# Latent attention in paired turns, weight splits and pool copies at other places, transposes for the modulation rows, and a negated maximum

## The reference, cut to what matters

```python
def mla_pool_mixer(hc, hl, ...):
    al = attention(ql, concat([kc, kl]), concat([vc, vl]))         # x: 256 queries, 512 keys
    ol = concat([al, multiscale_pool(pl[..., i_p:], w_pool, s_pool)]) @ w_out
    ac = attention(qc, kc, vc)                                     # context: 256 queries, 256 keys
    oc = concat([ac, multiscale_pool(pc[..., i_p:], w_pool, s_pool)]) @ w_out
def attention(q, k, v):
    s = einsum('bqhgd,bkhd->bhgqk', q, k) * scale
    return einsum('bhgqk,bkhd->bqhgd', softmax(s), v)
def first_block(...):
    h = h + rms_norm(y, g_mix_post[i]); u = rms_norm(h, g_ffn_pre[i])       # a "join"
    ml = (silu(c) @ w_mod[i] + b_mod[i]).reshape(B, N_MOD, 1, D)            # modulation
```

## Time and profile before

| what | value |
|---|---|
| median of three executions | 1772.74 us |
| the profiled execution, its own time | 1771.68 us |
| its span, first to last instruction | 1769.9 us |
| TensorE busy | 1672.9 us, 95% |
| VectorE busy | 1215.4 us, 69% |
| ScalarE busy | 918.9 us, 52% |
| mean granted TensorE clock | 0.989 |
| latent attention, first scores to first product behind it | 924.0 to 993.4 us |

### The profile page before, as it was taken

The page is one execution under the profiler, slowest core; times in us unless marked ns, Lnnn a source line. Parts: engine busy times, 40 slices in busy tenths (PEclk is TensorE's granted clock), DMA queues, the critical chain, the costliest instruction groups (busy, mean ns, idle before and its releaser), DMA issues.

```text
span 1769.9 us, 25025 instructions
## 1 busy us (share of the span) xinstructions
PE 1672.9 (95%) x9848; PEld 1414.4 (80%) x9848; DVE 1215.4 (69%) x1462; ACT 918.9 (52%) x1192; POOL 0.2 (0%) x4
## 2 busy tenths in 40 slices
PE   7978999999998899999988999999999988999998
PEld 6867888988876788898864668888888867789997
DVE  6956778777875777756567459777666656677754
ACT  6476664474437665467466453331234264665543
POOL 0000000000000000000000000000000000000000
PEclk9999999999999999999998999999999999999999
DMA  7812558745651466633140126446544522045551
GB/s 251 297 56 96 172 184 259 236 153 194 202 167 49 127 190 227 212 120 111 51 123 21 49 72 202 155 130 227 205 147 158 171 86 96 29 139 191 188 176 66
DMA packets 240471, 264.75 MB, mean 150 GB/s; under 512 B 7007, under 2 KB 218978, under 8 KB 240354
## 3 DMA queue, kind: packets, MB, share of 16 engines
q1 hardware_dynamic: 238428, 258.84, 44.9%
q10 hardware_dynamic: 1926, 4.32, 0.7%
HBM read 262.08 MB, written 1.05 MB: 149 GB/s over the span
## 4 chain that ended last, share of the span: by engine, by line
PE 75%; ACT 12%; DVE 10%; issue 2%; DMA 0%; ACTq 0%; DVEq 0%
PE ps L728 74%; DVE wlo L1822 2%; ACT whi L1203 2%; ACT y L1608 1%; DVE pr L2374 1%; ACT u L1611 1%; DVE small L2363 1%; DVE y L2125 1%; ACT pr L1753 1%; PE ps L1134 1%; ACT u L1399 0%; ACT y L1339 0%; ACT sbl L1714 0%; ACT sbe L1710 0%; ACT sbt L1708 0%
## 5 line engine op out<-in xcount | busy, mean ns | idle before, releaser
L728 PE MATMUL ps<-u,whi 128*128 128x512 f32 (+1 forms) x3472 | 895.1, 341 | 25.8 <-DVE wlo L1822 7.4
L728 PEld LDWEIGHTS ps<-u,whi 128*128 128x128 f32 x3472 | 596.5, 190 | 123.1 <-issue 23.5
L728 PE MATMUL ps<-u,wlo 128*128 128x256 f32 (+1 forms) x2116 | 648.9, 307 | 0.0
L1822 DVE TENSOR_TENSOR wlo<-raw,whi 128x2048 fp32r<-128x2048 f32 (+6 forms) x212 | 454.0, 2142 | 213.5 <-ACT whi L1203 206.0
L1203 ACT ACTIVATE whi<-raw 128x2048 fp32r<-128x2048 f32 (+6 forms) x212 | 380.7, 1796 | 221.3 <-PE ps L728 203.0
L728 PEld LDWEIGHTS ps<-u,wlo 128*128 128x128 f32 x2116 | 402.3, 190 | 19.7
L728 PE MATMUL ps<-hid,whi 128*128 128x512 f32 (+1 forms) x1212 | 353.6, 364 | 0.0
L728 PE MATMUL ps<-hid,wlo 128*128 128x256 f32 (+1 forms) x864 | 261.6, 303 | 0.0
L728 PEld LDWEIGHTS ps<-hid,whi 128*128 128x128 f32 x1212 | 216.3, 189 | 40.3 <-issue 3.4
L728 PEld LDWEIGHTS ps<-hid,wlo 128*128 128x128 f32 x864 | 163.4, 189 | 7.1
L2125 DVE SCALAR_TENSOR_TENSOR y<-idle_half,cc,y 128x1024 f32<-128x1024 f32 x70 | 90.0, 1285 | 5.3 <-DVE wlo L1822 0.5
(11 more groups left out here) (269 smaller groups left out, 1619.3 us busy)
## 6 DMA issues: line engine op xcount, KB each, us to landing
raw<-in_ffn_w_up SPq DMA_DIRECT2D x44, 1024.0 KB, 5.1
raw<-in_w_ff_in SPq DMA_DIRECT2D x32, 1024.0 KB, 5.3
raw<-in_w_ff_out SPq DMA_DIRECT2D x32, 1024.0 KB, 5.3
modw<-in_w_mod SPq DMA_DIRECT2D x112, 256.0 KB, 3.9
idle_half<-in_w_mod SPq DMA_DIRECT2D x80, 256.0 KB, 3.5
raw<-in_w_in_dil SPq DMA_DIRECT2D x18, 1024.0 KB, 5.1
raw<-in_w_in_sb SPq DMA_DIRECT2D x12, 1024.0 KB, 7.3
raw<-in_w_ple_gate SPq DMA_DIRECT2D x8, 1024.0 KB, 5.0
```

The source lines that it names most:

```text
L728: return pe.matmul(out_, lhsT, rhs, start=start, stop=stop, skip_group_check=True)
L1822: nc.vector.tensor_tensor(wlo[:, s % SPLIT, 0:n], raw[:, c["r"] % RAW, 0:n], whi[:, s % SPLIT, 0:n].bitcast(F32), ALU.subtract).then_inc(* ...
```

## The change

1. The matrix `select` goes; `mod_turn` makes four 128x128 transposes with the identity into the whole bank, and VectorE reads every 32nd column of it. The constants' DMA is a ninth smaller.
2. `late_splits`: the split three ahead of `uv`'s last chunk is left until behind the latent attention; so two splits wait there in place of one.
3. In a join whose waiting splits hold the second chunk of the next product (`second_chunk`), ScalarE makes that chunk's `whi` before the join's first step. This holds at three joins: behind `ff_out0`, `dil_out` and `ff_out1`. VectorE's order stays.
4. The pool's four banks are copied inside the latent attention, two behind the first round's exponentials and maxima, one in each of the next two rounds.
5. The latent attention's rounds alternate: context, x, context, x.
6. The score's scale is put into q (in the copy of `uq`, and in the gain of `gqa`'s q), so the exponential has none, and the maximum is written negated: L2365 goes, 48 times.

```diff
-    squares = np.concatenate([ident, ones, negtri, -ones, perm1, perm_m, perm_g, past, select], axis=1)
+    squares = np.concatenate([ident, ones, negtri, -ones, perm1, perm_m, perm_g, past], axis=1)
...
+            if p["kind"] == "linear" and p["name"] == "uv":
+                return [], [p["groups"][-1][-1]["s"] + SPLIT]
...
-            return [], [s + 2, s + SPLIT] if p["name"] == "dil_out" else [s + SPLIT]
+            return [], [s + 2, s + SPLIT] if p["name"] in ("dil_out", "pool_w") else [s + SPLIT]
...
+        def second_chunk(i):
+
+            if phases[i]["kind"] != "join":
+                return None
+            q = phases[i + 1] if phases[i + 1]["evac"] != "ple" else phases[i + 2]
+            return q["groups"][1][0]["s"]
...
-                n = 0
-                for seg in (1, 0):
-                    for pair in range(4):
-                        for q in range(2):
+                for pair in range(4):
+                    for q in range(2):
+                        for seg in (1, 0):
+                            n = 2 * pair + 1 - seg
...
-                    last = mm(ps[:, 6, 4 * j:4 * j + 4], modrow[:, j * P:(j + 1) * P], select, True, True)
+                    last = pe.transpose(ps[:, 6, j * P:(j + 1) * P], modrow[:, j * P:(j + 1) * P], ident)
...
-                    nc.scalar.activation(qm[0:96, 2 * g:2 * g + 2, :], A_[0:96], ACT.Copy).then_inc(*up("group_read_s", key))
+                    nc.scalar.activation(qm[0:96, 2 * g:2 * g + 2, :], A_[0:96], ACT.Copy, scale=MLA_HD ** -0.5).then_inc(*up("group_read_s", key))
...
+                    if second_chunk(i) in waiting_splits(i):
+                        split_high(second_chunk(i))
                     for g in range(4):
                         act.wait_ge(*at("tiles_ready", (i, g)))
...
                     for u in units[0:step]:
                         exp_(u)
+                    if p["what"] == "mla":
+                        pool_high(i, 0)
+                        pool_high(i, 1)
                     for n in range(0, N, step):
                         for u in units[n + step:n + 2 * step]:
                             exp_(u)
+                        if p["what"] == "mla" and n < 4:
+                            pool_high(i, 2 + n // 2)
...
+                gain_q = vec[:, ROW["gqa_g_q"]:ROW["gqa_g_q"] + 1]
+                dve.wait_ge(*own())
+                nc.vector.tensor_scalar(gain_q, gain_q, P ** -0.5, None, ALU.mult).then_inc(*up("vector_step"))
...
-                            nc.vector.tensor_reduce(small[:, 8 + b:9 + b], ps[:, n % 4, 0:W], AX.X, ALU.max).then_inc(*up("vector_step"))
-                            dve.wait_ge(*own())
-                            nc.vector.tensor_scalar(small[:, b:b + 1], small[:, 8 + b:9 + b], -u["scale"], None, ALU.mult).then_inc(
-                                *up("max_ready", (i, n)))
+                            nc.vector.tensor_reduce(small[:, b:b + 1], ps[:, n % 4, 0:W], AX.X, ALU.max, negate=True).then_inc(*up("max_ready", (i, n)))
...
+                    if p["what"] == "mla":
+                        pool_low(0)
+                        pool_low(1)
```

More of the change, by code:

```diff
@@ L73, in constants @@
     past = (i[:, None] < i[None, :]).astype(float)
-    select = np.zeros((P, P))
-    for q in range(4):
-        select[32 * q, q] = 1.0
-    squares = np.concatenate([ident, ones, negtri, -ones, perm1, perm_m, perm_g, past, select], axis=1)
+    squares = np.concatenate([ident, ones, negtri, -ones, perm1, perm_m, perm_g, past], axis=1)
     freq = np.zeros((P, 1))
@@ L183, in build @@
         small = sb("small", [P, 64])
-        ident, ones, negtri, negones, perm1, perm_m, perm_g, past, select = (squares[:, j, :] for j in range(9))
-        select = select[:, 0:4]
+        ident, ones, negtri, negones, perm1, perm_m, perm_g, past = (squares[:, j, :] for j in range(8))
         ps = ctx.enter_context(nc.psum_tensor("ps", [P, 8, 512], F32))
@@ L532, in build @@
         latent_i = next((p["i"] for p in phases if p["kind"] == "cnorm"), None)
+        pool_group = next((p["groups"][0][0]["gi"] for p in phases if p.get("evac") == "poolw"), None)
         entry_i = next((p["i"] for p in phases if p["kind"] == "entry"), None)
@@ L630, in softmax_units @@
                 u["n"] = n
-                u["ends"] = n + 1 == len(units) or units[n + 1]["pair"] != u["pair"]
+                u["ends"] = all(v["pair"] != u["pair"] for v in units[n + 1:])
             return units
@@ L1501, in evac @@
                 elif kind == "poolw":
-                    for t in range(4):
-                        act.wait_ge(*own())
-                        nc.scalar.activation(uh[:, 4 + t, :], ps[:, 4 + t, :], ACT.Copy, scale=vec[:, ROW["pool_scale_2"] + t:ROW["pool_scale_2"] + t + 1]).then_inc(
-                            *up("operand_high", (i, t)))
+                    pass
                 elif kind == "conv" and g % 2 == 0:
@@ L1524, in evac, with pool_high @@
                         hidden_high_conv(p, g)
+            def pool_high(i, t):
+                act.wait_ge(*own())
+                nc.scalar.activation(uh[:, 4 + t, :], ps[:, 4 + t, :], ACT.Copy, scale=vec[:, ROW["pool_scale_2"] + t:ROW["pool_scale_2"] + t + 1]).then_inc(
+                    *up("operand_high", ("pool", t)))
             def context_copied(q):
@@ L1752, in exp_ @@
                         act.wait_ge(*own())
-                        nc.scalar.activation(pr[:, n % 4, 0:W], src, ACT.Exp, scale=-1.0 if u["mask"] is not None else u["scale"], bias=small[:, b:b + 1], accum_out=small[:, 4 + b:5 + b]).then_inc(
+                        nc.scalar.activation(pr[:, n % 4, 0:W], src, ACT.Exp, scale=-1.0 if u["mask"] is not None else 1.0, bias=small[:, b:b + 1], accum_out=small[:, 4 + b:5 + b]).then_inc(
                             *up("weights_exp", (i, n)))
@@ L1801, in _ @@
                 for s in waiting_splits(i):
-                    split_high(s)
+                    if s != second_chunk(i):
+                        split_high(s)
         @block.vector
@@ L1919, in evac @@
                 elif kind == "poolw":
-                    for t in range(4):
-                        dve.wait_ge(*at("operand_high", (i, t)))
-                        sc = vec[:, ROW["pool_scale_2"] + t:ROW["pool_scale_2"] + t + 1]
-                        dve.wait_ge(*own())
-                        nc.vector.scalar_tensor_tensor(ul[:, 4 + t, :], ps[:, 4 + t, :], sc, uh[:, 4 + t, :].bitcast(F32), ALU.mult, ALU.subtract).then_inc(
-                            *up("group_read_v", ("pool", t)))
-                    C.note("group_read_v", key)
+                    pass
                 elif kind == "conv" and g % 2 == 0:
@@ L1953, in evac, with pool_low @@
                         hidden_low_conv(p, g)
+            def pool_low(t):
+                sc = vec[:, ROW["pool_scale_2"] + t:ROW["pool_scale_2"] + t + 1]
+                dve.wait_ge(*at("operand_high", ("pool", t)))
+                dve.wait_ge(*own())
+                nc.vector.scalar_tensor_tensor(ul[:, 4 + t, :], ps[:, 4 + t, :], sc, uh[:, 4 + t, :].bitcast(F32), ALU.mult, ALU.subtract).then_inc(
+                    *up("group_read_v", ("pool", t)))
+                C.note("group_read_v", ("group", pool_group))
             def conditioning():
@@ L2104, in mod_keep @@
                     dve.wait_ge(*own())
-                    nc.vector.tensor_tensor(dst[:, :, :, s_], sums[:, :, :, s_], base, ALU.add).then_inc(*up("mod_kept", st["i"]))
+                    nc.vector.tensor_tensor(dst[:, :, :, s_], sums[:, :, :, s_, 0], base, ALU.add).then_inc(*up("mod_kept", st["i"]))
                 for which in (1, 4):
@@ L2396, in _ @@
                             norm_(u)
+                        if p["what"] == "mla" and n < 4:
+                            pool_low(2 + n // 2)
                         if turned_first(n):
```

9 lines of the change are left out of this document (4 added, 5 removed).

## The result

The changed kernel takes 1756.5 us at the median (1754.8 to 1758.0, four runs) beside 1772.7 for the kernel before: a ratio of 0.9901, with a 95% interval from 0.9874 to 0.9929. That is 16.2 us less; the forecast was 1758.0. In a second set of five runs the same kernel gave 1757.7 and 0.9906 (0.9892 to 0.9921). The profiled execution has a span of 1753.5 us, 16.4 less than the 1769.9 of before.

The account below looks back on a forecast made before the run. TensorE, busy 95% of the span, was taken as the bound. Terms of -4.3, -1.7, -3.7, -4.2, -0.8 and -0.1 sum to -14.8 on the profiled 1771.7, 1756.9, or 1758.0 against the median; 80% range 1752 to 1766.

Parts of the forecast that it names:

- three joins: Behind `ff_out0`, `dil_out`, `ff_out1`: TensorE's 1.92 us wait for `wlo` goes, 0.5 comes back; 1.4 a join, -4.3 us.
- clock behind `dil_out`: With the join's wait gone, TensorE's granted clock stays at 1.00 right behind it: -1.7 us.
- modulation rows: Ten sets inside products: four transposes hold TensorE 0.44 us instead of 0.81, giving -3.7 us.
- latent attention: The whole stage, from its earlier first maximum, the removed scaling instruction and the alternating rounds: -4.2 us.
- grouped attention: TensorE sets the pace except in a few units; the missing scaling gives 0.19 us in each of these: -0.8 us.
- constants: 64 KB less of some 3 MB to load in the first 12 us, with x among it: -0.1 us.
- as much the other way wherever a shifted program meets a new dip: Bound on TensorE's clock term: up to 1.7 us lost per new low-clock stretch elsewhere, two of those allowed.
- the start: Latent attention's beginning: first maximum 6.2 us earlier, mostly paid back by pool copies inside the rounds: -1.2 us.
- the scaling: Latent attention: VectorE's removed scaling gives 0.19 us a unit over sixteen units, 3.0 us, between 1.5 and 4.7.
- the order: Latent attention's alternating 256- and 512-key rounds: slack gained set against waits before `low_`; 0, between -2.6 and +4.
- Rival C: Latent attention's alternating rounds lose: eight pair endings each hold VectorE about 1 us; +8 on the stage, 1766; chance 0.10.
- waits before `low_` over 10 us: Latent attention, VectorE: the prediction is wrong if these waits add up to over 10 us.

Follow-up runs that it names:

- experiment 9: The kernel before, with only `low_` of a finished pair moved behind the same step's two reciprocals and products on VectorE: 1770.9 us, ratio 0.9985.
- experiment 11: The changed kernel with the four pool copies and the uv split back ahead of the latent attention's first maximum: 1757.5 us, ratio 0.9911.
- 10: The changed kernel with the maximum and its change of sign as two VectorE instructions again, in both attentions: 1756.8 us, ratio 0.9911.
- 7: The changed kernel with the latent attention's rounds in the old order, all of the context's pairs first: 1758.7 us, ratio 0.9918.
- experiment 6: The changed kernel with `low_` of a finished pair moved behind the same step's two reciprocals and products on VectorE: 1751.1 us, ratio 0.9876.

## Why the prediction was right, step by step

The time, 1756.5, is 1.5 us from the forecast, and the profiled span moved by 16.4 where the sum said 14.8. The terms one by one, measured in the profiles:

| term | forecast | measured |
|---|---|---|
| three joins | -4.3 | -4.7 (1.5, 1.8, 1.4) |
| clock behind `dil_out` | -1.7 | -1.7 there; the whole span's dips 14.6 and 15.1 |
| modulation rows | -3.7 | -4.5; median -4.1 |
| latent attention | -4.2 | -5.0, of which 1.3 is a dip; -3.7 without it |
| grouped attention | -0.8 | -0.8 (39.44 to 38.65 us) |
| constants | -0.1 | -0.4 (wait for x 8.3, now 7.9) |

These add up to 17.1 beside the span's 16.4, and to 14.1 without the two dips, where the forecast without its clock term has 13.1. Either lies inside the interval of the medians (12.6 to 22.3 us less). So the mechanisms carry the result, but that the time came within 1.5 us of the forecast is partly luck: single dips and unchanged sections move a profile by more than that.

**The joins** went as argued: the wait of 1.92 is gone, and the late operand costs a part of a microsecond. Measured, 1.66 from the root to g1's first product in the first join. The forecast's 1.4 was low because less of the delay arrived: the operand came 0.63 later behind the root, but TensorE was ready for g1 15.19 us behind it before (377.25) and 15.45 now, 0.26 later.

**The clock** came out as forecast at the place it named, and in size (1.67). That the wait of 1.92 brings the dip is borne out by three profiles against three, and not without exception: experiment 9 has the wait and no dip behind it. The step "as much the other way wherever a shifted program meets a new dip" was needed too: in the two profiles of before and after the whole span's sum stayed the same, with the new dip at 578 and the longer one at 520. The Trainium skill says (TensorE: Matmul & The Clock Gate, Part 1: What's actually happening) that the number of slow matmuls at a start differs from run to run of one kernel, and advises against fitting to it. For the span as a whole the traces agree: 10.3 and 15.1 us in two profiles of one program.

**The modulation rows** were undersized because I priced four transposes at the 0.44 of the earlier trace rows, from the grouped attention. In the middle of a product they cost 0.36, and in nine of the ten sets of the changed kernel (0.43 in the tenth). Why it is less there was not tested.

**The latent attention.** Its parts were forecast at -1.2 for the start, -3.0 for the scaling and 0 for the order; experiments 11, 10 and 7 show about -2.1, -2.4 and 0, which is 0.8 more than the 3.7 that the stage gave without the dip; taken out one at a time from the changed kernel, they need not add up. The start was undersized: the sum had the first product 2.9 sooner and 1.7 of it paid back by the last two pool copies; by experiment 11 the first transposes come 3.3 sooner (10.31 less 7.02 us behind the first scores), and 2.0 to 2.3 of that is left, so that those copies cost 1.0 to 1.3. The scaling was oversized, because the waits ahead of `low_` swallow part of what VectorE saves; the forecast named those waits, but charged them to the order alone. Rival C's mechanism was therefore real, but not the new order's alone: the waits are 10.1 us now, 10.5 with the old order and 8.0 in the kernel before (6.6 in its execution without the dip), which paid for them too, though only 2.7 us (experiment 9). It seems that more of them stood on the path once the scaling was gone; no run takes that apart.

The signs that the prediction set were met: no wait for `wlo` at the joins, operand 2.1 behind the root, a set at 0.36, VectorE's first product of the latent attention 6.61 us behind the first scores where it was 9.73, the stage 5.0 shorter. One warning sign, waits before `low_` over 10 us, was reached as well (10.1), and experiment 6 shows what it was worth: 5.8 us. As a sign that the forecast is wrong it was badly placed, since the kernel before stood at 8.0 already.

## What to carry to other kernels

Where an in-order engine has a consumer's step standing ahead of the next round's step, look at the idle time printed before it: moving the call behind work that is ready gave 5.8 us here, more than the four other edits in that stage together (5.0). An instruction taken from an engine is worth its time only if nothing behind it waits for another engine; see which wait swallows it. And read a part from its own stretch, since whole spans of one program differ by more than most of its parts, and look for a dip of the clock in it first: 1.3 of this stage's 5.0 us was one.

## What the runs showed of the hardware that I had not expected

Matmuls ran at two paces at the same granted clock. In the unchanged linear product from 184 to 280 us TensorE is busy throughout at 1.00, and the same instructions take 399 and 281 ns in one profile, 394 and 277 in another. First the kernel before, then the one with the transposes alone:

```profile
L728 PE MATMUL ps<-u,whi 128*128 128x512 f32 x235 | 83.1, 399 | 0.0
L728 PE MATMUL ps<-u,wlo 128*128 128x256 f32 x235 | 66.0, 281 | 0.0
```
```profile
L728 PE MATMUL ps<-u,whi 128*128 128x512 f32 x230 | 79.8, 394 | 0.0
L728 PE MATMUL ps<-u,wlo 128*128 128x256 f32 x231 | 64.0, 277 | 0.0
```

The section from the root at 182 to the one at 362 is 176.4 to 176.8 us in six profiles and 178.8 to 179.5 in eight, with both lengths in either group of the table above. The section from 599 to 783 does the same: without a dip behind the join it is 181.0 to 181.5 us in seven profiles and 183.4 to 184.5 in four, and the profile of the changed kernel has the long form of the one section and the short form of the other, so the pace changes within an execution. Other sections (47.91 to 47.93 from 831 to 879; 197.36 to 197.38 ahead of the last root) do not scatter at all. What sets the pace was not tested.

Four float32 transposes of 128x128 in succession hold TensorE 0.36 us inside a product, less than half of what four products of 4 columns, run as eight passes, hold it (0.81).
